# One projection block moved ahead of a scan step's outputs, more expert rows summed on TensorE during the top-k, and pooled doublings cut to each group's own window

## The reference, cut to what matters

```python
proj = h @ w_in                      # pool values | z | x,B,C | dt | gate_pool | gate_ssm
a_out = pool_mixer(...)              # 4 groups of 256 channels, trailing windows 2, 4, 8, 16:
                                     #   (window sum / count) - self, then a 256x256 map, then a scale
m_out = ssm_mixer(...)               # conv, chunked scan (chunks of 128), gate, grouped RMSNorm, out_w
h = layer_norm(DN_ALPHA * h + (sigmoid(g_pool) * a_out + sigmoid(g_ssm) * m_out) @ w_out)
# PEER: 8 heads, each picks 16 of 128*128 experts by two top-16 searches over 128 keys
h_k = einsum('td,thkd->thk', x, expert_u[idx])          # 128 dots a token
act = gelu(h_k) * softmax(scores)
out = einsum('thk,thkd->td', act, expert_v[idx])        # 128 weighted rows a token
h = layer_norm(DN_ALPHA * h + out)
```

## Time and profile before

| | us |
|---|---|
| median of 3 runs | 3926.68 |
| lowest and highest of them | 3921.19, 3930.45 |
| the profiled execution | 3919.56 |
| its span, first to last instruction | 3917.5 |
| TensorE busy, of the span | 3098.7 |
| VectorE busy | 3043.0 |
| GpSimd busy | 2108.0 |
| ScalarE busy | 923.6 |

### The profile page before, as it was taken

The page is one execution under the profiler, slowest core; times in us unless marked ns, Lnnn a source line. Parts: engine busy times, 40 slices in busy tenths (PEclk is TensorE's granted clock), DMA queues, the critical chain, the costliest instruction groups (busy, mean ns, idle before and its releaser), DMA issues. The chain is left out here.

```text
span 3917.5 us, 39965 instructions
## 1 busy us (share of the span) xinstructions
PE 3098.7 (79%) x12052; PEld 2225.5 (57%) x12052; DVE 3043.0 (78%) x8003; ACT 923.6 (24%) x2201; POOL 2108.0 (54%) x1839
## 2 busy tenths in 40 slices
PE   8999963899987777999898767998887766565665
PEld 7888852677776445777676435776775432121221
DVE  4442289878887899888877999888877898677667
ACT  3332102244412112344312112343311111011101
POOL 0000014667766667676665677766665667555553
PEclk9999986899998898999998888999998887786877
DMA  4333347999999999999999999999999999999997
GB/s 160 108 113 126 143 155 250 337 375 395 399 397 402 326 376 366 383 394 399 399 380 397 346 366 375 377 395 368 385 375 397 328 335 356 422 422 421 422 422 327
DMA packets 306565, 1333.72 MB, mean 340 GB/s; under 512 B 34352, under 2 KB 38832, under 8 KB 249008
## 3 DMA queue, kind: packets, MB, share of 16 engines
q0 software_dynamic: 262656, 1073.86, 71.0%
q1 hardware_dynamic: 42400, 252.61, 16.4%
q10 hardware_dynamic: 1296, 4.72, 0.3%
HBM read 1326.85 MB, written 4.19 MB: 340 GB/s over the span
## 5 line engine op out<-in xcount | busy, mean ns | idle before, releaser
L432 POOL DMA_INDIRECT rowbuf<-eu,idx x800 | 902.2, 1128 | 1002.0 <-DVE idx L1382 535.9
L1401 DVE CUSTOM_DVE_ANT_0 rowbuf<-rowbuf,hb 128x1024 f32<-128x1024 f32 x884 | 1078.0, 1220 | 155.2 <-DMA rowbuf<-eu,idx 79.9
L432 POOL DMA_INDIRECT rowbuf<-ev,idx x800 | 918.6, 1148 | 485.6 <-PE vbank L549 231.6
L549 PE MATMUL vbank<-rowbuf,vdiag 128*128 128x512 f32 x1340 | 750.4, 703 | 354.5 <-ACT vdiag L851 237.9
L471 PE MATMUL main<-xT,ring 128*128 128x256 f32 x3584 | 795.8, 382 | 79.1 <-ACT mm L894 67.2
L471 PEld LDWEIGHTS main<-xT,ring 128*128 128x128 f32 x3584 | 688.5, 192 | 182.5 <-issue 87.9
L1426 DVE SCALAR_TENSOR_TENSOR acc<-rowbuf,hact,acc 128x1024 f32<-128x1024 f32 x549 | 705.1, 1284 | 101.9 <-DMA rowbuf<-ev,idx 93.7
L549 PEld LDWEIGHTS vbank<-rowbuf,vdiag 128*128 128x128 f32 x1340 | 281.4, 223 | 742.3 <-issue 409.6
L851 ACT ACTIVATE vdiag<-ident,hact 128x128 f32<-128x128 f32 x417 | 149.1, 393 | 468.1 <-DVE hact L1409 463.6
L654 PE MATMUL main<-late,ring 128*128 128x256 f32 x1024 | 233.0, 390 | 21.1 <-issue 15.3
L471 PE MATMUL main<-early,ring 128*128 128x256 f32 x1024 | 232.6, 387 | 0.7 <-ACT early L1014 0.7
(11 more groups left out here) (227 smaller groups left out, 3433.1 us busy)
## 6 DMA issues: line engine op xcount, KB each, us to landing
ring<-wblocks SPq DMA_DIRECT2D x224, 1024.0 KB, 8.1
rowbuf<-eu,idx POOLq DMA_INDIRECT x800, 8.5
rowbuf<-ev,idx POOLq DMA_INDIRECT x800, 8.4
xT<-xt SPq DMA_DIRECT2D x4, 1024.0 KB, 17.1
pw<-poolw SPq DMA_DIRECT2D x16, 256.0 KB, 8.2
zy<-x SPq DMA_DIRECT2D x4, 1024.0 KB, 12.7
h_out<-acc ACTq DMA_DIRECT2D x8, 512.0 KB, 7.8
craw_ln<-ln1g SPq DMA_DIRECT2D x4, 512.0 KB, 15.2
```

Of the source, the lines that this page charges most:

```text
L432: pool.indirect_dma_start(rows[r], None, (eu, ev)[table], bass.IndirectOffsetOnAxis(ap=idx[c % 2][:, u, k:k + 1], axis=0)).then_inc(row_re ...
L549: last = pe.matmul(vbank[half][:, :], vdiag[:, n % DIAGS, :], r[:, half * 512:(half + 1) * 512], start=first, stop=False, skip_group_check ...
L1401: last = dve.tensor_tensor_reduce(r, r, hb[c % 2][:, t, :], 1.0, 0.0, ALU.mult, ALU.add, hdot[:, g % 2, k:k + 1])
```

## The change

Three edits, on the same inputs and with the same outputs.

```diff
@@ share_of_pe
     if off < ATD:
         return 0.4
-    return 0.75
+    return 0.75 if off < ATD + 30 else 1.0
@@ front_a2 on TensorE
                 for s in range(4):
                     if s < 3:
                         scan_scores(c, j, s + 1)
                     until(o + (22, 25, 28, 30)[s])
-                    scan_outputs(c, j, s)
                     if s == 0:
                         w = block_in(c, j * (8 // RING), 7)
                         tokens(bank(c, j * MA, 9), w, xT).then_inc(block_done, 1)
+                    scan_outputs(c, j, s)
@@ pooling on VectorE
-                for w in range(4):
+                for w in range(j + 1):
                     lo = 2 * reach - 1
                     dve.tensor_tensor(dst_[:, :, lo:E], src[:, :, lo:E], src[:, :, lo - reach:E - reach], ALU.add)
                     dve.drain()
-                    fixed = dst_[:, :, HALO:E]
...
-                    src, dst_, reach = dst_, (psb if dst_ is psa else psa), 2 * reach
-                    yield
+                    if w < j:
+                        src, dst_, reach = dst_, (psb if dst_ is psa else psa), 2 * reach
+                        yield
+                start = 0
+                if first:
+                    start = 16
+                    fixed = yt1[:, 0:32].rearrange("p (a t) -> p a t", a=2)
+                    dve.tensor_tensor(fixed, dst_[:, :, HALO:HALO + 16],
+                                      pfix[:, j, :].unsqueeze(1).to_broadcast([P, 2, 16]), ALU.mult)
+                    dve.drain()
+                    dve.scalar_tensor_tensor(out=pooled[:, :, 0:16], in0=fixed, scalar=1.0 / WINDOWS[j],
+                                             in1=praw[:, :, HALO:HALO + 16], op0=ALU.mult, op1=ALU.subtract)
+                dve.scalar_tensor_tensor(out=pooled[:, :, start:T], in0=dst_[:, :, HALO + start:E], scalar=1.0 / WINDOWS[j],
+                                         in1=praw[:, :, HALO + start:E], op0=ALU.mult, op1=ALU.subtract
+                                         ).then_inc(pool_done, 1)
+                dve.drain()
+                yield
```

More of the change, by code:

```diff
@@ L157, in build @@
         iota = sb("iota", [P, NCAND])
-        pcoef = sb("pcoef", [P, 4, 4])
         pfix = sb("pfix", [P, 4, 16])
@@ L1167, in pooling @@
-                    if w == 3:
-                        last.then_inc(pool_done, 1)
-                    dve.drain()
-                    src, dst_, reach = dst_, (psb if dst_ is psa else psa), 2 * reach
-                    yield
+                    if w < j:
[7 more added lines that the diff above has]
+                                      pfix[:, j, :].unsqueeze(1).to_broadcast([P, 2, 16]), ALU.mult)
+                    dve.drain()
+                    dve.scalar_tensor_tensor(out=pooled[:, :, 0:16], in0=fixed, scalar=1.0 / WINDOWS[j],
+                                             in1=praw[:, :, HALO:HALO + 16], op0=ALU.mult, op1=ALU.subtract)
@@ L1518, in _ @@
             dve.sem_inc(topk_done, 2)
-            dve.memset(pcoef[:, :, :], 0.0)
             dve.memset(ctail[:, :, :], 0.0)
@@ L1523, in _ @@
             dve.drain()
-            for w in range(4):
-                dve.memset(pcoef[:, w, w:w + 1], 1.0 / WINDOWS[w])
             dve.wait_ge(const_made, 11)
```

## The result

The changed kernel takes 3938.5 us (median of 9 runs, 3934.2 to 3944.0) where the kernel before, in the same series, takes 3924.7 (9 runs, 3919.4 to 3930.5): a ratio of 1.0034, 95% interval 1.0023 to 1.0044, or 13.9 us slower. That lies in the range of the prediction (3898 to 3950), and outside the likeliest case's own range (3916 to 3938) by half a microsecond: its sum said +1, the chip says +14. The profiled execution took 3940.5 us, span 3938.4.

A forecast was written before the change was run, and what follows sets the result against it. No engine bounds the whole: DVE paces the top-k from offset 202, and groups are TensorE's front plus DVE's tail. Terms -42 + 19 + 39 - 2 - 13 = +1 on 3926.7 gave about 3928 us, range 3898 to 3950.

The forecast's parts named there:

- The forecast's own case: Whole kernel: terms cancel within 8 us, about 3928 us, own range 3916 to 3938; chance 0.42.
- More V rows on TensorE, -42: Top-k from offset 202: 13, 13 and 14 rows leave DVE, saving 42 us of at most 51.
- the DMA ... is hardly slack either: Top-k stretch: the DMA needs 145 us against the 149 us that DVE would need.
- The planner's carry, +19: Group ends: V rows at offset 31 delay TensorE; their new places cost 19 us, ends +9 and +24.
- Block 7, +39: Scan of c = 1..3: DVE waits 4.4 us for outputs, 3.25 us net in twelve groups, 39 us.
- the stall is absorbed: Rival: next groups' scans wait for rows, so block 7's 39 becomes 5; 3894 us, a quarter.
- The -2 in c = 0: Block 7's move in the groups without retrieval: DVE's 0.7 us product is hidden, -2 over four groups.
- Pooling, -13: Shorter pooling saves 13 us of DVE per superchunk; gains 4.4 us in three A0 groups, 13 us.
- TensorE's gain ends where DVE or its rows come last: A0 scan: DVE stood only 4.54 us before it in c = 2, limiting pooling to 4.4 us a group.
- Faster: Outcome for the whole kernel, from the cases of absorbed stall and fully counting pooling; chance 0.30.
- TensorE late in the top-k: Rival: TensorE bounds the ten steps with query blocks, 25 us saved for 42; about 3950 us, a fifth.
- The 358 GB/s: Rival: the skill's HBM limit for a core already fills the top-k stretch, no gain there; 3970 us, 3%.

The follow-up runs named there:

- e_share: Kernel before with only the share of V rows on TensorE raised to 1.0 from offset 202: 3909.3 us, ratio 0.9966.
- e_share_no31: Kernel before with share 1.0 from offset 202 and no V row of TensorE at a group's offset 31: 3915.6 us, ratio 0.9884.
- first series: Runs of each part alone and the change without block 7's move, beside the kernel before at 3926.5 us.
- e_share_pool: The changed kernel without block 7's move, against the kernel before: 3903.9 us, ratio 0.9946; repeated on another chip: 3973.5 us, ratio 1.0000.
- third series: Later runs on another chip, repeating kernels with and without the planner rule; the kernel before took 3974.3 us there.
- offset-31 rule: Planner edit to the kernel before or others: no V row falls to TensorE at a group's last step; alone 0.9933, again 0.9938.
- second series: Runs of kernels with no V row of TensorE at offset 31, same chip as the earlier runs; the kernel before took 3962.0 us.
- e_no31: Kernel before with only the planner edit that keeps V rows off TensorE at a group's offset 31: 3939.2 us, ratio 0.9933.

## Why the prediction was right in its range, and where its sum missed

The range held, but its three outcomes did not fare well: "slower", by more than the 8 us that a measurement can tell, is what came, and it had the least chance of the three, 0.28. The forecast's own case was "same".

**More V rows on TensorE, -42: the mechanism right, the size a little more, and a consequence missing.** The first stretch came to 151.5 us from 166.6, and the three to -45 in all (-46 in `e_share`). TensorE did not fall behind as the rival had it: PE's granted clock rose to 0.98 and it waited for rows in 27 places, though POOL waits 11.0 us for it. The missed step is in "the DMA ... is hardly slack either". I used it as a bound on the gain and did not follow it to the next stage. POOL issues in order, some 1.35 us an issue (111.7 us busy and 26.5 us between issues for 102 rows). Before, it was held up by DVE for 22.6 us, so it was ahead, by 10 rows at the end of the top-k. After, it is at its own pace, issues 101 or 102 rows in the stretch where it issued 106, and A0 begins with a lead of 5 or 6. At the last step of the third top-k, 39 rows were still to issue for 34. The next stage pays: +13.8 us of the 46 in `e_share`, where DVE waits for rows in c2 A0 for the first time; and where the lead stayed at 10, in `e_share_no31`, it does not pay. That the lead is the cause rests on these traces; no run gave it back with all else kept. The measured term is -32.

**The planner's carry, +19: right**, +18.8, with the waits for a diagonal of 8.7 to 9.9 us at the ends of c2 A1 and A2, and none at c2 A3, as forecast. `e_share_no31` bears out the cause by taking it away, in full for c2 A2 and in part for c2 A3. The term's lower end is summed wrongly: one of the two hidden gives 11.7 - 4.5 = 7, not 9.

**Block 7, +39: right.** 4.46 us of wait where the text said 4.4, the 1.15 given back, and +34.6 in company, +44.6 alone. The rival "the stall is absorbed" is out for the whole; it holds in one group, c2 A0, where rows come last. The -2 in c = 0 can't be told: that superchunk ended at 653.6 us for 653.8, but at 656.1 in `e_share`, which changes nothing in it.

**Pooling, -13: right alone** (-12.6, in the A0 groups), **probably less in company.** The step that failed is the one that treated it as independent of the first term. I wrote that "TensorE's gain ends where DVE or its rows come last", and took the bound of 4.54 us from the trace of before; after the first edit rows come last in c2 A0 and c3 A0. Some 7 us of the 13 go by the medians, which the ratios alone can't tell from none; the stage lengths put them in these two groups.

The corrected sum for the first series: -46 + 19 + 14 for the share (-13; the medians say -17), -13 + 7 for the pooling and +35 for block 7. With the medians' -17 that is +12, where the change measured +14. This sum is no check of its own, since the 7 and the 35 are taken from the differences of these same kernels. The forecast had the same with -23, -13 and +37. So it missed by 6 to 10 us in the first term and some 7 in the pooling, the other way by 2 to 4 in block 7, and that the last took back a part is luck. "Faster" fell because little was absorbed; "slower" came true by a path that none of the rivals named: a faster stage that eats the lead of the next. The rival that did say slower, TensorE late in the top-k, is summed wrongly too: 3928 + 17 + 10 to 20 is 3955 to 3965, not "about 3950", so the range that was to hold it ends below it.

*The 358 GB/s:* the changed stretch moved 379 GB/s, and the first series' `e_share_pool` 380, so the stretch of before was not full. (The 358 of the third series' stretch is 4% more bytes than the first's 380, in 10% more time.) The rival from the Trainium skill, "DMA: Bandwidth & Descriptors", section on bandwidth, is out by these rows. That section also says of its measured figures that they are for a core whose neighbour is idle, and gives each core the 358 only with both streaming; this kernel runs on one core, and I read the rule without that condition.

**What beats both.** The change without block 7's move is the fastest of the first series (-22.6, and -34.6 against the change). The offset-31 rule gains in each of the three pairs that stood in one series. Beyond that no kernel leads: in the second series the share with the rule is as fast with the pooling as without (0.9878 and 0.9884), and in the third the rule alone is as fast as the rule with share and pooling (0.9938 and 0.9943). In the quick conditions of the first series the rule was not run.

## What to carry to other kernels

Ask of a stage that you make faster what it was storing up for the next: where a producer in a fixed order (here the gathers) was held back by the slow consumer, its lead is spent first; here 14 of 46 us of the gain were paid in the following stage. Prices of two edits that meet in the same stage need not add: by the medians the share and the pooling lost a quarter together, in the stages where both act. And a unit of work moved ahead of the first link of a chain costs its length less the slack of that one link, every time it is passed (7 us of matmuls, some 3 us of time, twelve times), even when it leaves the engine's own total as it was.

## What the runs showed of the hardware that was not expected

The gain in the top-k, where the DMA engines are busy for 0.96 to 1.0 of the time, depended on the series: the same kernel's stretch took 151 us in the first and 166 in the third, with engines idle for nothing that the profile shows. In the kernels that leave DVE the slower engine (`e_no31`, 166.8 us in the second series for 166.6 in the trace of before) the same stretch did not change. A verdict on such an edit taken in one series would be wrong in another: 0.9946 and 1.0000 for one kernel.

The first superchunk, which has no retrieval beside it for the most part, was longer too: it ended at 661 to 664 us in the second and third series, and at 654 to 659 in the traces of the quick times.
